# Hybrid mLSTM and window-attention decoder step on one Trainium2 core: turning the key and value tiles behind the first qo chunks in place of between two stages

## The reference

```python
proj = xn @ w_in                          # q, k, v, o and the gates
b = jnp.cumsum(lf, axis=-1)
d = jnp.where(causal, b[..., :, None] - b[..., None, :] + ig[..., None, :], -jnp.inf)
...
s = jnp.einsum('bhtk,bhsk->bhts', q, k) * jnp.exp(d - m_t[..., None])
num = w_inter[..., None] * jnp.einsum('bhtk,bhkv->bhtv', q, C) + jnp.einsum('bhts,bhsv->bhtv', s, v)
...
C_new = w_old[..., None, None] * C + jnp.einsum('bhs,bhsk,bhsv->bhkv', w_s, k, v)
```

## Time and profile before

| | |
|---|---|
| median of 3 runs | 1465.06 us (1462.29 to 1467.04) |
| profiled execution, its own time | 1466.03 us |
| span of the profiled execution | 1464.2 us |
| busy share of TensorE, VectorE, ScalarE | 95%, 60%, 40% |
| TensorE's share of the chain that ended last | 85% |
| granted clock over the span | 0.979 |

### The profile page before, as it was taken

How to read it: one execution, slowest core, us unless ns; L and a number is a source line. 1 busy time by engine, 2 the same in 40 slices (tenths; PEclk the granted TensorE clock), 3 DMA queues, 4 the chain that set the end, 5 groups by cost and what they waited for, 6 DMA issues and landing times.

```text
span 1464.2 us, 25626 instructions
## 1 busy us (share of the span) xinstructions
PE 1395.0 (95%) x11019; PEld 1345.6 (92%) x11019; DVE 876.8 (60%) x1613; ACT 579.0 (40%) x1017; POOL 35.3 (2%) x61
## 2 busy tenths in 40 slices
PE   6999999999999999999899888899999999999987
PEld 6989977999999999999799866799999999999977
DVE  4444666587777774224785647667777777432464
ACT  5122244554444442225451135654444444322441
POOL 2000110000000000001000000000000000000000
PEclk9999999999999999999999968999999999999999
DMA  7332641212223333224122210121223233322212
GB/s 230 101 87 59 203 143 58 87 45 73 87 87 102 87 95 118 99 90 141 58 88 87 78 44 1 71 85 48 58 88 101 87 90 103 121 83 96 75 58 92
DMA packets 33794, 131.91 MB, mean 90 GB/s; under 512 B 4149, under 2 KB 4237, under 8 KB 33281
## 3 DMA queue, kind: packets, MB, share of 16 engines
q1 hardware_dynamic: 28368, 110.35, 23.6%
q0 software_dynamic: 5312, 19.91, 4.4%
HBM read 121.61 MB, written 10.05 MB: 90 GB/s over the span
## 4 chain that ended last, share of the span: by engine, by line
PE 85%; DVE 10%; ACT 2%; issue 2%; DMA 1%; SPq 0%; POOL 0%; DVEq 0%; ACTq 0%
PE tile L838 22%; PE tile L842 22%; PE tile L840 22%; PE tile L848 3%; PE tile L849 3%; PE tile L850 3%; PE side L1241 1%; PE sums L879 1%; DVE sm L1852 1%; DVE wL L1321 1%; DVE soft L1867 1%; DVE cv L1346 1%; ACT wH L507 1%; PE side L848 1%; PE side L850 1%
## 5 line engine op out<-in xcount | busy, mean ns | idle before, releaser
L507 ACT ACTIVATE wH<-raw 128x1024 fp32r<-128x1024 f32 (+1 forms) x193 | 214.3, 1111 | 470.1 <-DMA raw<-in_w_up 146.9
L838 PE MATMUL tile<-xH,wH 128*128 128x260 f32 x1872 | 380.9, 285 | 16.7 <-DVE xL L1393 10.4
L842 PE MATMUL tile<-xH,wL 128*128 128x260 f32 x1872 | 378.7, 284 | 0.0
L840 PE MATMUL tile<-xL,wH 128*128 128x260 f32 x1872 | 378.5, 284 | 0.0
L1321 DVE TENSOR_TENSOR wL<-raw,wH 128x1024 fp32r<-128x1024 f32 (+1 forms) x193 | 249.2, 1291 | 175.6 <-ACT wH L507 171.3
L838 PEld LDWEIGHTS tile<-xH,wH 128*128 128x128 f32 x1872 | 290.5, 189 | 20.7 <-issue 17.4
L842 PEld LDWEIGHTS tile<-xH,wL 128*128 128x128 f32 x1872 | 290.4, 190 | 0.0
L840 PEld LDWEIGHTS tile<-xL,wH 128*128 128x128 f32 x1872 | 289.6, 189 | 0.0
L1361 DVE TENSOR_TENSOR u<-tile,rstd 128x520 f32<-128x520 f32 x102 | 71.3, 699 | 155.1 <-PE tile L842 155.0
L838 PE MATMUL tile<-hidH,wH 128*128 128x260 f32 x616 | 124.1, 283 | 0.0
L842 PE MATMUL tile<-hidH,wL 128*128 128x260 f32 x616 | 123.8, 282 | 0.0
(11 more groups left out here) (322 smaller groups left out, 1961.2 us busy)
## 6 DMA issues: line engine op xcount, KB each, us to landing
raw<-in_w_up SPq DMA_DIRECT2D x88, 512.0 KB, 3.6
raw<-in_w_down SPq DMA_DIRECT2D x32, 704.0 KB, 4.0
raw<-in_w_ple SPq DMA_DIRECT2D x16, 512.0 KB, 3.6
raw<-in_w_kv SPq DMA_DIRECT2D x13, 512.0 KB, 3.7
raw<-in_w_qo SPq DMA_DIRECT2D x12, 512.0 KB, 3.6
raw<-in_w_qkv SPq DMA_DIRECT2D x12, 512.0 KB, 3.6
cring<-in_c_in POOLq DMA_DIRECT2D x8, 512.0 KB, 4.4
out_c_s<-cring POOLq DMA_DIRECT2D x8, 512.0 KB, 3.6
```

Of the source, the lines that this page charges most:

```text
L507: nc.scalar.activation(wH[j][:, 0:n], raw[j][:, 0:n], ACT.Copy).then_inc(s_high, 1)
L838: nc.tensor.matmul(out[:, q, 0:HT], wh, x[0][:, k, tokens(q)], start=first, stop=False)
L840: nc.tensor.matmul(out[:, q, 0:HT], wh, x[1][:, k, tokens(q)], start=False, stop=False)
L842: mm = nc.tensor.matmul(out[:, q, 0:HT], wl, x[0][:, k, tokens(q)], start=False, stop=last)
```

## The change

The twelve turns leave the place between the stages. The column products come first, and behind each of the first four qo chunks three tiles are turned. The copies on VectorE and ScalarE move with them, behind that chunk's scaled read and weight split. The stacks are built in parts: the keys' behind chunk 1, the values' in two halves behind chunks 2 and 3, the first mask behind chunk 3. `diag` moves from chunks 0 and 4 to 4 and 7, `decays` from 1 and 5 to 5 and 8.

```diff
@@ -576,10 +576,6 @@
             act.wait_ge(s_rows, 1)
             nc.scalar.activation(erow, brow[:], ACT.Exp, scale=-1.0).then_inc(s_rexp, 1)
             nc.scalar.activation(srow[:], srow[:], ACT.Exp).then_inc(s_rexp, 1)
-            for i in range(1, 3 * NH, 2):
-                act.wait_ge(s_turn, i + 1)
-                nc.scalar.activation(turned_to(i)[0], side[:, 1, :].rearrange("p (b c) -> p b c", b=NB),
-                                     ACT.Copy).then_inc(s_tra, 1)
             act.wait_ge(s_dml, 1)
             nc.scalar.activation(wcol[:], wcol[:], ACT.Exp).then_inc(s_wcol, 1)
 
@@ -598,6 +594,11 @@
                     at0 += SEQ - j * P
                 last.then_inc(s_expd, 1)
 
+            def turn_read(i):
+                act.wait_ge(s_turn, i + 1)
+                nc.scalar.activation(turned_to(i)[0], side[:, 1, :].rearrange("p (b c) -> p b c", b=NB),
+                                     ACT.Copy).then_inc(s_tra, 1)
+
             def numerators(n):
                 for i, b in enumerate(reversed(range(NB))):
                     e = (NB + 1) * n + i
@@ -614,8 +615,12 @@
 
             for c in range(COUNT["qo"]):
                 high(*ahead("qo", c + 2))
-                if c in (1, 5):
-                    decays(c // 4)
+                if c < NH:
+                    for i in range(3 * c, 3 * c + 3):
+                        if i % 2:
+                            turn_read(i)
+                if c in (5, 8):
+                    decays(c // 8)
 
             act.wait_ge(s_read, READ0["mout"])
             for k in range(0, KT, 4):
@@ -909,10 +914,8 @@
                 chunk("kv", c, X)
 
 
-            for i in range(3 * NH):
-                if i == 0:
-                    pe.wait_ge(s_read, READ0["qo"])
-                    pe.wait_ge(s_root, 1)
+            def turn_tile(i):
+
                 if i >= 2:
                     pe.wait_ge(s_trd if i % 2 == 0 else s_tra, i // 2)
                 if i >= 4 and i % 4 == 0:
@@ -922,6 +925,8 @@
                     mm = nc.tensor.transpose(side[:, i % 2, b * P:b * P + P], kvq[:, i, b * P:b * P + P], ident)
                 mm.then_inc(s_turn, 1)
 
+            pe.wait_ge(s_read, READ0["qo"])
+            pe.wait_ge(s_root, 1)
             pe.wait_ge(s_rexp, 2)
             for b in range(NB):
                 nc.tensor.matmul(sums[:, 1, NH * b:NH * b + NH], cv[0:NH, b * P:b * P + P], ident[0:NH, 0:NH],
@@ -963,7 +968,10 @@
             for c in range(COUNT["qo"]):
                 free_after("qo", c)
                 chunk("qo", c, X)
-                if c >= NH:
+                if c < NH:
+                    for i in range(3 * c, 3 * c + 3):
+                        turn_tile(i)
+                else:
                     sample_products(c - NH)
 
             st_at = [(0, 0), (0, 512), (1, 0), (1, 256)]
@@ -1436,17 +1444,6 @@
                 low(*ahead("kv", c + 2))
                 if c == 0:
                     kv_rows()
-            for i in range(0, 3 * NH):
-                if i % 2 == 0:
-                    dve.wait_ge(s_turn, i + 1)
-                    nc.vector.tensor_copy(turned_to(i)[0], side[:, 0, :].rearrange("p (b c) -> p b c", b=NB)
-                                          ).then_inc(s_trd, 1)
-                if i % 4 == 3:
-
-                    dve.wait_ge(s_turn, i + 1)
-                    dst = (ktoks, vtoks, vtoks)[i // 4][:].rearrange("b n d -> b (n d)")
-                    c = (i // 8) * 512
-                    nc.vector.tensor_copy(dst[:, c:c + 512], sums[0:DEC, 0, :]).then_inc(s_tsr, 1)
             dve.wait_ge(s_cols, 1)
             chain.did(nc.vector.tensor_copy(acol[:].rearrange("p b n -> p (b n)"), sums[:, 1, 0:16]))
             chain.did(nc.vector.tensor_copy(wscol[:], sums[0:DEC, 1, 16:16 + NH]))
@@ -1456,18 +1453,36 @@
             chain.link(nc.vector.tensor_scalar(rs[:, 0, 0:NH], sums[:, 1, 128:128 + NH], 1.0, None, ALU.mult))
             nc.vector.tensor_tensor(wcol[:], acol[:], rs[:, 0, 0:NH].unsqueeze(1).to_broadcast([P, NB, NH]),
                                     ALU.subtract).then_inc(s_dml, 1)
-            dve.wait_ge(s_tsr, 3)
-            chain.link(nc.vector.tensor_tensor(vtoks[:], vtoks[:], wscol[:].unsqueeze(2).to_broadcast([DEC, NH, DV]),
-                                               ALU.mult))
 
             dve.wait_ge(s_zero, 2)
-            for rows in (slice(0, DEC), slice(32, 32 + DEC)):
-                chain.did(nc.vector.tensor_scalar(kst[rows], ktoks[:], 1.0, None, ALU.mult))
-            for rows in (slice(0, DEC), slice(64, 64 + DEC)):
-                chain.did(nc.vector.tensor_scalar(vst3[rows], vtoks[:], 1.0, None, ALU.mult))
-            dve.wait_ge(s_dve, chain.n)
-            chain.did(nc.vector.tensor_tensor(kst[64:64 + DEC], ktoks[:], kst[0:DEC].bitcast(F32), ALU.subtract))
-            chain.link(nc.vector.tensor_tensor(vst3[32:32 + DEC], vtoks[:], vst3[0:DEC].bitcast(F32), ALU.subtract))
+
+            def turn_read(i):
+                dve.wait_ge(s_turn, i + 1)
+                if i % 2 == 0:
+                    nc.vector.tensor_copy(turned_to(i)[0], side[:, 0, :].rearrange("p (b c) -> p b c", b=NB)
+                                          ).then_inc(s_trd, 1)
+                if i % 4 == 3:
+                    dst = (ktoks, vtoks, vtoks)[i // 4][:].rearrange("b n d -> b (n d)")
+                    c = (i // 8) * 512
+                    nc.vector.tensor_copy(dst[:, c:c + 512], sums[0:DEC, 0, :]).then_inc(s_tsr, 1)
+
+            def stack_keys():
+                dve.wait_ge(s_tsr, 1)
+                for rows in (slice(0, DEC), slice(32, 32 + DEC)):
+                    chain.did(nc.vector.tensor_scalar(kst[rows], ktoks[:], 1.0, None, ALU.mult))
+                dve.wait_ge(s_dve, chain.n)
+                chain.link(nc.vector.tensor_tensor(kst[64:64 + DEC], ktoks[:], kst[0:DEC].bitcast(F32), ALU.subtract))
+
+            def stack_values(half):
+                n = slice(2 * half, 2 * half + 2)
+                dve.wait_ge(s_tsr, 2 + half)
+                chain.link(nc.vector.tensor_tensor(vtoks[:, n], vtoks[:, n],
+                                                   wscol[:, n].unsqueeze(2).to_broadcast([DEC, 2, DV]), ALU.mult))
+                for rows in (slice(0, DEC), slice(64, 64 + DEC)):
+                    chain.did(nc.vector.tensor_scalar(vst3[rows, n], vtoks[:, n], 1.0, None, ALU.mult))
+                dve.wait_ge(s_dve, chain.n)
+                chain.link(nc.vector.tensor_tensor(vst3[32:32 + DEC, n], vtoks[:, n], vst3[0:DEC, n].bitcast(F32),
+                                                   ALU.subtract))
 
             def mask(b):
                 if b >= 2:
@@ -1552,12 +1567,20 @@
                     nc.vector.tensor_tensor(xL[:, k, :], o_tile(k), xH[:, k, :].bitcast(F32), ALU.subtract
                                             ).then_inc(s_xr, 1)
 
-            mask(0)
             for c in range(COUNT["qo"]):
                 scaled_read("qo", c, kvq[:, c + 3 * NH if c < NH else c, :])
                 low(*ahead("qo", c + 2))
-                if c in (0, 4):
-                    diag(c // 4)
+                if c < NH:
+                    for i in range(3 * c, 3 * c + 3):
+                        turn_read(i)
+                if c == 1:
+                    stack_keys()
+                if c in (2, 3):
+                    stack_values(c - 2)
+                if c == 3:
+                    mask(0)
+                if c in (4, 7):
+                    diag(c // 7)
                 if c >= NH:
                     new_memory(c - NH)
 
```

## The result

The changed kernel is slower: 1469.83 us, median of 22 runs, against 1466.05 for the kernel before, also 22 runs. The ratio is 1.0029 with a 95% interval of 1.0018 to 1.0040, that is +4.3 us (2.6 to 5.9). Single runs spread more than before: 1463.65 to 1474.35 against 1462.20 to 1470.86. They fall into two groups, 5 of 22 from 1463.65 to 1464.63 and 17 from 1468.02 to 1474.35; the granted clock was 0.980 in the five and 0.975 to 0.976 in the seven slowest. The profiled execution (1469.62 us) has a span of 1467.8 us, granted clock 0.978.

What follows compares the result with a forecast made beforehand. TensorE, busy 95% of the span, was taken to bound the kernel. Stalls of +3.2 us and one further clock spell of +1.6 made +4.8, taking the median from 1465.1 to 1469.9 us, range 1466.3 to 1473.0.

Steps and rivals of the forecast that it cites:

- within 0.3%: Outcome band for the median: no spell, the rest of one spell, most of the not-slower case; chance 0.43.
- steps 1 to 3: Edge and first four qo chunks: turns removed there, three added behind each chunk with waits for readers; +3.2 us.
- the bare sum: Edge plus four boundaries without clock effects: 14.99 us before, 4.82 + 12.55 + 0.80 = 18.17 after, 3.2 us more.
- steps 4 to 6: qo stage: stacks in parts stay hidden, moved diag and decays fit idle time, DMA is not delayed; cost 0.
- step 7: Clock: first qo chunk's spell unchanged, one further spell behind the new idles; 1.6 us, bounds 0 and 3.2.
- I leave a spell of the same price there: First qo chunk: its slow-clock spell costs 1.6 us as before, so no difference.
- the two long idles: TensorE idles of 2.34 and 2.40 us behind qo chunks 1 and 2; one on average costs a spell, 1.6 us.
- Not slower: Rival: VectorE's copies run ahead of the weight split, three boundaries lose 1.23 us less each; -0.5 us, 1464.6; chance 0.08.
- No further slow spell: Rival: behind the new idles the clock does not fall, stalls cost 3.2 us and that is all; 1468.3; chance 0.30.
- both long idles: Rival: both idles behind qo chunks 1 and 2 drop the clock; +6.4 us, 1471.5; chance 0.20.
- A second stall: Rival: moved stacks, masks or later cring loads also delay sample products, some 0.5 us at several places; over +8; chance 0.06.

Runs made afterwards that it cites:

- experiment 1: Changed kernel with VectorE's copies of the turned tiles ahead of the weight split behind the first four qo chunks: 1465.75 us, ratio 1.0003 to the kernel before.
- experiment 2: Changed kernel with one more 128x1024 subtraction on VectorE between weight split and copies, behind each of the first four qo chunks: 1476.6 us, ratio 1.0077.
- experiment 4: Kernel before with only diag moved to chunks 4 and 7 and decays to 5 and 8, turns left between the stages: 1465.58 us, ratio 0.9995.
- experiment 6: Changed kernel with all parts of the stacks built behind chunk 3 in place of behind chunks 1, 2 and 3: 1470.97 us, ratio 1.0047.
- copies_first: The same run as experiment 1: changed kernel, copies ahead of the weight split; 1465.75 us, ratio 1.0003.
- stacks_late: The same run as experiment 6: changed kernel, all stacks built behind chunk 3; 1470.97 us, ratio 1.0047.
- double_split: The same run as experiment 2: changed kernel, an extra subtraction between split and copies; 1476.6 us, ratio 1.0077.
- kv_turns_cols: Kernel before with one turn behind each kv chunk from the third, and column products in two parts behind kv chunks 7 and 9: 1458.26 us, ratio 0.9950.
- cols_first: Kernel before with the column products put ahead of the twelve turns, both still between the stages: 1465.38 us, ratio 1.0004.

## Why the prediction was right, step by step

**The number.** The forecast median, 1469.9, and the measured one, 1469.83, agree more closely than the forecast deserves. It started from a median of three runs that lay 1.0 us below that of 22, and it added 4.8 us, where the medians moved by 3.8 and the ratio says 4.3 (2.6 to 5.9). The stalls, 3.2 of the 4.8, were worked out; that the clock's 1.6 came near is luck, as below. The change is +0.29%, so it fell in the band that the forecast called within 0.3%, to which it gave 0.43 against 0.52; only the 22 runs tell it from none.

**The stalls (steps 1 to 3).** Right in place, cause and size. From the changed kernel's read of qo chunk 0 to that of chunk 4 pass 36.41 us, before 23.07: +13.3, forecast 12.55 plus 0.80, 13.35 (the four chunks themselves are in both). At the edge the first product started 1.06 us behind the read (forecast 0.95) and the rest of its working holds except for the clock: 15.62 less the spell's 4.7 is 10.9, forecast 10.79. So the bare sum is +3.3 against +3.2. Experiments 1 and 2 show the cause: the wait for VectorE follows the work ahead of the copies down and up.

**The moved and split work (steps 4 to 6).** Right: experiment 4 shows diag and decays free, experiment 6 shows what the stacks' cover was worth (2.6 us) and that it held, with 1.4 us to spare where 0.9 was forecast.

**The clock (step 7).** The size of the sum came out near, the place, as far as the profile shows, did not. I had left the spell at the first qo chunk at its old price and put one further spell behind an idle of 2.3 us. In the profile after no spell lay behind 2.19 and 2.31 us, nor behind 2.8 and 3.3 in experiment 2; the extra cost sat in the step "I leave a spell of the same price there". That term was forecast 0 and measured +3.1 us (4.7 against 1.6) in the one profiled execution, because the spell lasted 10.2 us in place of 3.4 and the small products that lie in it take twice as long too. It is no single case: the three other versions with the same program up to the first qo read took 15.76, 15.67 and 14.05 us for the edge in their profiles (copies_first, stacks_late, double_split), which is 4.9, 4.8 and 3.2 more than the 10.9 without a spell. Why it lasts longer there isn't shown. What I charged for the two long idles, 1.6, measured 0 in this profile; with double_split's other runs in view it may not be 0 in every execution. The medians hold less of it: 4.3 us in all less 3.3 for the stalls leaves 1.0 for the clock, with an interval of -0.7 to 2.6. What share of executions has the long spell isn't measured; the two groups of single runs, with their granted clocks, say only that the executions differ by the clock.

**The profiled pair.** Its spans differ by 3.6 us only, though the qo stage ends 7.2 late (last qo read 195.70 before, 202.94 after). The changed kernel starts its first stage 0.8 us late, which is no part of the change, and later falls of the clock lie elsewhere: by the first read of the up stage (302.69 and 308.24) 1.7 us are given back, as the spell that before lay at 203 us is absent, and by the end another 2.0. That the pair agrees with the medians in total rests on this give and take; what the change itself does was to be read from the intervals inside the two stages.

**The rivals.** "Not slower" is out for the changed kernel by its copies' waits, and in as experiment 1: with the copies ahead the ratio is 1.0003, +0.4 us with an interval from -1.5 to 2.5, forecast -0.5. The Trainium skill ("TensorE: Matmul & The Clock Gate", section "Architectural detail: the array is 16× 32×32, not 1× 128×128") has VectorE's queue strictly in order, and the traces agree: in experiments 1 and 2 the copies' time followed what stood ahead of them, down and up. "No further slow spell" and "both long idles" are neither confirmed: in the profile the first is right about the idles, wrong about the clock as a whole. "A second stall" is out: no wait ahead of a sample product.

The Trainium skill, "TensorE: Matmul & The Clock Gate", section "HAM oscillation — how this bites in real kernels", tells of a kernel that waited for DMA behind each short group of matmuls and began the next one at half clock, and advises a loop order that keeps TensorE at full clock. No wait here is for a DMA, but the traces agree with the aim: in kv_turns_cols, with turns and products spread among dense chunks and one wait of 0.2 us, the granted clock is 1.00 from 60 to 140 us.

## What to carry to other kernels

Here, moving small work into a dense stage paid only where its readers weren't waited for. So look at what stands ahead of the reader in its own queue, here a read and a split of 1.9 us, met once before and at three boundaries of four after. One double-buffered piece behind each chunk, with a whole chunk's time for its reader, cost its own 0.51 us; three at once behind a chunk, with two banks, needed a bank back at once and waited 1.6 to 2.3 us at three boundaries of four. Count each boundary from rows that already show the same sequence; that gave 9.1, 9.8, 9.8 and 7.7 us to within 0.1.

## What the runs showed that I had not expected

- A fall of the clock takes small products with it: pairs 4 columns wide went from 0.21 to 0.42 us, the transposes of a turn from 0.54 to 1.07. I had taken such work for bound by issue and so free of the clock.
- Where TensorE didn't wait, a spell cost a little under half its length whatever lay in it: 3.4 us at half clock cost 1.6 in a dense chunk, 6.8 cost 3.2 (double_split) and 10.2 cost 4.7 over products and chunk. In cols_first, where turns in the spell waited for their readers anyway, 13.6 us cost some 4.7 (the first qo matmul starts 19.75 us behind the last kv read in place of 14.99).
- In the profiled executions idles of 2.2, 2.3, 2.6, 2.8 and 3.3 us among dense chunks were followed by full clock, one of 3.4 by half; in the earlier trace rows half clock followed 2.26 behind sparser work, and at 104.8 us of the changed kernel an idle of 1.1 and small products. The idle's length alone does not tell.
